# Two attention layers: transposes of a pair's first head ahead of the next pair's scores, softmax weights one block earlier

## The chip, the cores and the metric

The kernel runs on one core of one Trainium2 chip. The metric is the device time of one execution in microseconds (us), median of three runs. The profile is of one more execution on the same core.

## What is computed

A sequence of 16 meta tokens and 256 tokens of width 1024 goes through a first block (feed-forward, an mLSTM mixer, feed-forward) and then through two layers of a second block. The change is in these two layers, which are alike:

```python
for l in range(DEPTH_2):                       # 2 layers
    h = rms_norm(x, pre_norm_g[l]) * (1.0 + scale[:, None, :]) + shift[:, None, :]
    proj = h @ w_in[l]                          # q, k, v, g_att, u, b_gate, c_gate, g_conv
    ...
    att = dilated_attention(q, k, v, rel_bias).astype(h.dtype) * jax.nn.silu(g_att)
    cnv = b_gate * short_conv(c_gate * u, conv_w[l]) * jax.nn.silu(g_conv)
    mix = jnp.concatenate([att, cnv], axis=-1) @ w_out[l]
    x = x + gate[:, None, :] * rms_norm(mix, post_norm_g[l])
```

The dilated attention has 8 heads of 64. Its three windows are folded into one table of biases, so that each head is a softmax over 256 keys: scores, plus bias, exponential, division by the row sum, times v. Everything is float32.

## The kernel before, in words

Activations lie transposed, features on partitions and tokens along the free axis. Each large product is done in three TensorE passes on float32 operands that were split into a high part (`u1`, `w1`) and a low part (`u2`, `w2`). The weights stream from HBM in chunks of 128x1024 (512 KB): SP issues the load into one of five `raw` buffers, ScalarE casts the high part into `w1`, VectorE subtracts it to get the low part `w2`. `advance`, which runs inside `block`, issues cast and subtraction for the chunk that is used four blocks later; there are five buffers of each.

A `block` is one chunk times the normalised activations: 24 matmuls of 128x128 by 128x256 that sum in one of four PSUM banks taken in turn. After q, k and v, the loop that the change touches runs 21 steps, `at_` from 0 to 20; each of steps 0 to 19 has one block: the four gates of the attention first, then for each of four conv groups the blocks u, c_gate, b_gate and g_conv. ScalarE and VectorE empty each block's bank (`sg`, `cu`, `cw`).

Between the blocks stands the attention, by pairs of heads. `k = at_ // 4` counts the pairs and `part = at_ % 4` the step in a pair's four:

- `scores(k)`: TensorE multiplies q and k of both heads into PSUM banks 4 and 7. VectorE adds the bias (`Sb<-ps,Bt`) and takes the row maximum (`st<-Sb`). ScalarE takes four exponentials, and reads four row sums (`Sb,st<-Sb,st` and the accumulator reads).
- `weights2(k)`: VectorE takes the reciprocals of the sums (`st<-st`), GpSimd multiplies them in, two operations for each head (`Sb<-Sb,st`).
- `transposes(h)`: TensorE transposes one head's weights into PSUM bank 5 (`ps<-cs,Sb`), and ScalarE copies them to `PT`. It waits for the weights of the head and for bank 5, which the copy of the head before it frees.
- `values(k)`: TensorE multiplies the transposed weights of both heads by v, and VectorE applies the gate (`at`). `split_mix` then makes high and low parts of it (`m`), the high one on ScalarE, the low one on GpSimd.

In the four steps of pair k (from pair 1 on) TensorE therefore gets: scores of pair k, transposes of the first head of pair k-1, a block; transposes of its second head, a block; a block; `values(k-1)`, a block. Pair 4 has no scores, only the rest of pair 3.

No scheduler moves anything. Every call appends to one list for each engine, and each engine works its list in that order; a wait in a list holds all that stands behind it. A wait whose mark was already waited for is left out. All operations are issued from the lines in `replay`: L112 is an operation that no one waits for, L114 one that raises its engine's semaphore. So rows are told apart by the tiles that they name, not by lines.

Of the kernel before, what the change touches and what calls it, by code (L numbers as in the profile page):

```python
# [116 lines left out]
def build(nc, xT, wst, wada, vec, cst, tab, rb, outT):  # L117
    ctx = ExitStack()
    with ctx:
        def sb(name, shape, dt=F32, c=ctx):  # L120
            return c.enter_context(nc.sbuf_tensor(name, shape, dt))
# [27 lines left out]
        part = sb("part", [P, 96])  # L149
# [117 lines left out]
        def block(x1, x2, n, mid=None, marks=None, ahead=True):  # L267

            if ready:
                return ready.pop(0)  # L270
            b = take()
            c = chunk(ahead)
            pe.wait(free[b])
            for kt in range(KT):
                if marks:
                    pe.wait(marks[kt])
                if mid and kt == KT - 2:
                    mid()
                m = tile_products(ps[:, b, 0:n], c, kt, x1[:, kt, :], x2[:, kt, :], kt == 0, kt == KT - 1,
                                  kt == KT - 1)  # L280
            done_chunk(c, m)
            return b, m
# [822 lines left out]
        def layer(l, ygm, hm):  # L1105
# [51 lines left out]
            def silu2(dst, b, m, w, wr=None):  # L1157

                a = act(partial(nc.scalar.activation, w, ps[:, b, 0:S], ACT.Tanh, scale=0.5), m, wr)
                q = free[b] = dve(partial(nc.vector.scalar_tensor_tensor, dst, w, 1.0, ps[:, b, 0:S], ALU.add,  # L1160
                                                                         ALU.mult), a)
                return q

            def scores(k):


                pe.wait(free[4], free[7], qm[k], qm[4 + k])
                for t in range(2):
                    for e in range(2):
                        hp, b = 64 * e, 4 + 3 * e  # L1170
                        ms = pe(partial(nc.tensor.matmul, ps[:, b, S * t:S * t + S],
                                        qk[hp:hp + 64, k, 128 * t:128 * t + 128], qk[hp:hp + 64, 4 + k, :],
                                        start=True, stop=True))
                dve.wait(ms, br_m["w"])
                for e in range(2):
                    h, i, b = 2 * k + e, (2 * k + e) % 4, 4 + 3 * e
                    dve(partial(nc.vector.scalar_tensor_tensor, Sb[:, i, 0, :], ps[:, b, 0:S], 0.125,
                                Bt[:, h, 0:256], ALU.mult, ALU.add), sbr[i])
                    m = free[b] = dve(partial(nc.vector.scalar_tensor_tensor, Sb[:, i, 1, :], ps[:, b, S:2 * S],
                                              0.125, Bt[:, h, 128:384], ALU.mult, ALU.add))  # L1180
                    m = dve(partial(nc.vector.tensor_reduce, st_[:, i, 0:2], Sb[:, i, :, :], AX_X, ALU.max,
                                    negate=True), m)
                    for t in range(2):
                        x = act(partial(nc.scalar.activation, Sb[:, i, t, :], Sb[:, i, t, :], ACT.Exp,
                                        bias=st_[:, i, t:t + 1], accum_out=st_[:, i, 2 + t:3 + t]), m)
                    ex[h] = x

            def weights2(k):
                for h in (2 * k, 2 * k + 1):
                    i = h % 4  # L1190
                    r_ = dve(partial(nc.vector.reciprocal, st_[:, i, 4:6], st_[:, i, 2:4]), ex[h])
                    for t in range(2):
                        nrm[h] = pool(partial(nc.gpsimd.tensor_scalar, Sb[:, i, t, :], Sb[:, i, t, :],
                                              st_[:, i, 4 + t:5 + t], None, ALU.mult), r_)

            def transposes(h):
                i = h % 4
                pe.wait(free[5], nrm[h])
                for j in range(2):
                    for t in range(2):  # L1200
                        mt = pe(partial(nc.tensor.transpose, 
                            ps[:, 5, S * j + 128 * t:S * j + 128 * t + 128], Sb[:, i, t, 128 * j:128 * j + 128],
                            ident))
                sbr[i] = mt
                ptm[h] = free[5] = act(partial(nc.scalar.copy, PT[:, h % 2, :, :],
                                                          ps[:, 5, :].rearrange("p (j q) -> p j q", q=S)),
                                   mt, ptr[h % 2])

            def values(k):


                pe.wait(ptm[2 * k], ptm[2 * k + 1], mV, free[6])
                for j in range(2):
                    for e in range(2):
                        h, hp = 2 * k + e, 64 * e
                        mo = pe(partial(nc.tensor.matmul, ps[hp:hp + 64, 6, 0:S], Vt[:, j, 64 * h:64 * h + 64],
                                        PT[:, e, j, :], start=j == 0, stop=j == 1, skip_group_check=True))
                ptr[0] = ptr[1] = mo
                dve.wait(mx.get(k - 2))
                m = free[6] = dve(partial(nc.vector.scalar_tensor_tensor,   # L1220
                    at[:, k % 2, :], sg[:, k, :], 0.5, ps[:, 6, S - 1::-1], ALU.mult, ALU.mult), mo, sgm[k])
                todo.append(partial(split_mix, k, at[:, k % 2, :], m))
# [16 lines left out]
            wr = None  # L1239
            for at_ in range(21):  # L1240
                k, part = at_ // 4, at_ % 4
                if part == 0 and k < 4:
                    scores(k)
                if part == 2 and k < 4:
                    weights2(k)
                if part in (0, 1) and 0 < k < 5:
                    transposes(2 * k - 2 + part)
                if part == 3 and 0 < k:
                    values(k - 1)
                while todo:  # L1250
                    todo.pop(0)()
                if at_ == 20:
                    while todo:
                        todo.pop(0)()
                    break
                b, m = block(x1, x2, S)
                if at_ < 4:
                    sgm[at_] = wr = silu2(sg[:, at_, :], b, m, cw_[:, 4, :], wr)
                    continue
                j, part = (at_ - 4) // 4, (at_ - 4) % 4  # L1260
                cwt = lambda tap: vc[:, V_CW2 + 12 * l + 4 * tap + j:V_CW2 + 12 * l + 4 * tap + j + 1]
                if part == 0:
                    cm["u"] = free[b] = act(partial(nc.scalar.copy, cw_[:, 0, :], ps[:, b, 0:S]), m, cm.get("cu"))
                elif part == 1:
                    cm["cu"] = free[b] = dve(partial(nc.vector.tensor_tensor, cu[:, 1:S + 1], cw_[:, 0, :],
                                                     ps[:, b, 0:S], ALU.mult), m, cm["u"], cm.get("t"))
                    m = dve(partial(nc.vector.tensor_scalar, cw_[:, 1, :], cu[:, 0:S], cwt(0), None, ALU.mult),
                            cm["cu"])
                    m = dve(partial(nc.vector.scalar_tensor_tensor, cw_[:, 1, :], cu[:, 1:S + 1], cwt(1),
                                    cw_[:, 1, :], ALU.mult, ALU.add), m)  # L1270
                    cm["t"] = dve(partial(nc.vector.scalar_tensor_tensor, cw_[:, 1, :], cu[:, 2:S + 2], cwt(2),
                                          cw_[:, 1, :], ALU.mult, ALU.add), m)
                elif part == 2:
                    cm["b"] = free[b] = dve(partial(nc.vector.scalar_tensor_tensor, cw_[:, 2, :], cw_[:, 1, :], 0.5,
                                                    ps[:, b, 0:S], ALU.mult, ALU.mult), m, cm["t"], cm.get("x"))
                else:
                    dve.wait(cm.get("p"))
                    wr = silu2(cw_[:, 3, :], b, m, cw_[:, 4, :], wr)
                    m = cm["p"] = pool(partial(nc.gpsimd.tensor_tensor, cw_[:, 2, :], cw_[:, 2, :], cw_[:, 3, :],
                                               ALU.mult), wr, cm["b"])  # L1280
                    cm["x"] = None
                    todo.append(partial(split_conv, j, m))
# [102 lines left out]
```

How the kernel before makes its waits and increments, by code:

```python
    def replay(self, eng):  # L107
        for fn, m in self.ops:
            if fn is None:
                eng.wait_ge(m[0], m[1])
            elif m is None:
                fn()
            else:
                fn().then_inc(m[0], m[1])
```

## Time and profile before

| what | value |
|---|---|
| median of 3 runs | 833.57 us (833.28 to 833.63) |
| profiled execution | 833.62 us, of which the span from first to last instruction is 831.7 us |
| TensorE busy | 803.1 us, 97% of the span |
| VectorE busy | 584.6 us, 70% |
| ScalarE busy | 418.5 us, 50% |
| GpSimd busy | 128.0 us, 15% |
| DMA, all 16 engines | 56.7% of the span for the weights' queue |

Busy times are those of the profile; TensorE's matmuls overlap at their ends, so that the start-to-start distance of two rows says more than the duration of one. A number in square brackets at the end of a row is the time that the engine stood idle ahead of it, and behind the arrow stands what ended that time.

### The profile page before, as it was taken

The page shows a single profiled execution, that of the slowest core. Times are in us where ns is not written, and L with a number is a line of the kernel's source. Part 1 is how long each engine was busy: PE and PEld are TensorE (multiplying, and loading weights), DVE is VectorE, ACT ScalarE, POOL GpSimd, SP SyncE. Part 2 cuts the span into 40 slices and gives each one's busy share as a digit, 9 for nine tenths or more (in the row PEclk, how much of TensorE's full clock was granted, in tenths as well). Part 3 has the DMA queues.
Part 4 walks back from the last instruction along what each step waited for, and adds up shares of the span by engine and source line. Part 5 has one row for each costly group of instructions (what it writes and reads, how often), then busy time and mean ns, then how long its engine had stood idle before and what let it go on. Part 6 is the DMA issues. An engine that isn't in the chain of part 4 may idle for free.

```text
span 831.7 us, 15721 instructions
## 1 busy us (share of the span) xinstructions
PE 803.1 (97%) x6436; PEld 777.6 (93%) x6436; DVE 584.6 (70%) x946; ACT 418.5 (50%) x716; POOL 128.0 (15%) x138
## 2 busy tenths in 40 slices
PE   7999999999999999999999999999999999999996
PEld 7999999999899899999999999989888999898895
DVE  6777776798687875788777768775666468566543
ACT  7544444445257665555444454445654365464541
POOL 3000000032210000010000012220235202025413
PEclk9999999999999999999999999999999999999998
DMA  9876676776245632459888775517444451734421
GB/s 326 295 254 221 226 249 242 226 274 201 88 143 185 196 112 93 152 186 340 291 287 270 275 238 185 184 51 256 150 124 150 154 173 55 259 130 147 131 76 51
DMA packets 45751, 158.96 MB, mean 191 GB/s; under 512 B 5064, under 2 KB 7624, under 8 KB 45680
## 3 DMA queue, kind: packets, MB, share of 16 engines
q1 hardware_dynamic: 45680, 157.96, 56.7%
q8 instruction: 51, 0.84, 0.4%
q14 instruction: 20, 0.16, 0.1%
HBM read 156.88 MB, written 1.06 MB: 190 GB/s over the span
## 4 chain that ended last, share of the span: by engine, by line
PE 76%; DVE 14%; ACT 6%; issue 2%; DMA 1%; POOL 1%; SPq 0%; DVEq 0%; ACTq 0%; POOLq 0%
PE ps L112 69%; PE ps L114 7%; DVE w L114 3%; ACT w L114 2%; DVE u L114 2%; DVE tmp L114 2%; DVE yg L114 1%; DVE Sb L114 1%; DVE st L114 1%; DVE cv L114 1%; ACT SW L114 1%; ACT Sb L114 1%; ACT L114 1%; DMA raw<-wst 1%; POOL rst L114 1%
## 5 line engine op out<-in xcount | busy, mean ns | idle before, releaser
L112 PE MATMUL ps<-u,w 128*128 128x256 f32 (+1 forms) x3887 | 499.9, 285 | 3.1 <-DVE w L114 1.6
L112 PEld LDWEIGHTS ps<-u,w 128*128 128x128 f32 x3887 | 481.9, 188 | 11.3 <-DVE w L114 4.0
L114 DVE TENSOR_TENSOR w<-raw,w 128x1024 fp32r<-128x1024 f32 x245 | 297.4, 1225 | 168.0 <-ACT w L114 161.6
L114 ACT CAST w<-raw 128x1024 fp32r<-128x1024 f32 x245 | 254.8, 1050 | 135.5 <-PE ps L114 124.8
L112 PE MATMUL ps<-h,w 128*128 128x272 f32 (+1 forms) x1000 | 130.4, 285 | 0.0
L112 PEld LDWEIGHTS ps<-h,w 128*128 128x128 f32 x1000 | 126.1, 188 | 0.1
L114 POOL TENSOR_TENSOR sqa<-sqa,sq 128x256 f32<-128x256 f32 (+1 forms) x22 | 23.1, 1050 | 358.3 <-ACT sq L114 357.8
L114 POOL TENSOR_SCALAR Sb<-Sb,st 128x256 f32<-128x256 f32 x32 | 42.9, 1355 | 111.1 <-DVE st L114 111.1
L114 DVE SCALAR_TENSOR_TENSOR acc<-adr,cact,acc 128x1024 f32<-128x1024 f32 x42 | 56.4, 1353 | 0.3 <-DMA adr<-wada 0.3
L114 PE MATMUL ps<-u,w 128*128 128x256 f32 (+1 forms) x169 | 48.1, 284 | 0.0
L112 PE MATMUL ps<-m,w 128*128 128x256 f32 x368 | 46.7, 281 | 0.0
L112 PEld LDWEIGHTS ps<-m,w 128*128 128x128 f32 x368 | 44.8, 188 | 0.0
L114 ACT ACTIVATE sq<-ps 128x256 f32<-128x256 f32 (+1 forms) x37 | 14.4, 390 | 40.4 <-PE ps L114 40.4
L114 PEld LDWEIGHTS ps<-u,w 128*128 128x128 f32 x169 | 32.1, 190 | 0.0
L114 POOL TENSOR_TENSOR rst<-sst,eps 128x2 f32<-128x2 f32 (+2 forms) x7 | 5.6, 802 | 164.3 <-DVE sums L114 155.7
L114 DVE TENSOR_TENSOR hf<-si,ps 128x272 f32<-128x272 f32 (+1 forms) x44 | 18.9, 428 | 15.9 <-ACT si L114 11.4
L114 ACT ACTIVATE si<-tmp 128x272 f32<-128x272 f32 x22 | 9.5, 431 | 38.4 <-DVE tmp L114 38.4
L112 PE MATMUL ps<-y,w 128*128 128x256 f32 x184 | 24.6, 285 | 1.5 <-ACT ytm L114 1.5
L114 ACT ACTIVATE Sb<-Sb,st 128x256 f32<-128x256 f32 x32 | 16.0, 502 | 17.6 <-DVE st L114 17.6
L112 PEld LDWEIGHTS ps<-y,w 128*128 128x128 f32 x184 | 22.8, 188 | 1.7 <-ACT ytm L114 1.7
L114 POOL TENSOR_TENSOR hT<-hT,yg 128x256 f32<-128x256 f32 (+1 forms) x27 | 20.4, 756 | 22.3 <-DVE yg L114 22.3
L114 ACT ACTIVATE si<-ps 128x256 f32<-128x256 f32 x22 | 8.3, 383 | 30.6 <-PE ps L114 29.5
(175 smaller groups left out, 692.2 us busy)
## 6 DMA issues: line engine op xcount, KB each, us to landing
raw<-wst SPq DMA_DIRECT2D x245, 512.0 KB, 4.6
adr<-wada SPq DMA_DIRECT2D x48, 512.0 KB, 4.0
Bt<-bias_rows SPq DMA_DIRECT2D x8, 192.0 KB
hT<-xT SPq DMA_DIRECT2D x4, 272.0 KB, 4.9
outT<-hT SPq DMA_DIRECT2D x2, 384.0 KB, 2.6
outT<-hT SPq DMA_DIRECT2D x1, 256.0 KB, 2.6
cs<-cst SPq DMA_DIRECT2D x1, 140.0 KB, 6.3
cs<-cst SPq DMA_DIRECT2D x1, 128.0 KB, 7.2
```

The source lines that it names most:

```text
L112: fn()
L114: fn().then_inc(m[0], m[1])
```

## The change

It moves two calls in the loop. `transposes` for parts 0 and 1 now stands ahead of `scores`, and `weights2(k)` is called at part 1 rather than part 2, behind the transposes and ahead of the block of that step.

```diff
             for at_ in range(21):
                 k, part = at_ // 4, at_ % 4
+                if part in (0, 1) and 0 < k < 5:
+                    transposes(2 * k - 2 + part)
                 if part == 0 and k < 4:
                     scores(k)
-                if part == 2 and k < 4:
+                if part == 1 and k < 4:
                     weights2(k)
-                if part in (0, 1) and 0 < k < 5:
-                    transposes(2 * k - 2 + part)
                 if part == 3 and 0 < k:
                     values(k - 1)
```

No operation is added or taken away. On TensorE, at the first step of pairs 1, 2 and 3 in each layer, the order of the transposes (`ps<-cs,Sb`) and the scores (`ps<-qk`) is turned; the other rows are blocks:

```order
 L112 MATMUL ps<-u,w 128x256 x23
 L114 MATMUL ps<-u,w 128x256
+L114 MATMUL ps<-cs,Sb 128x128 x4
 L114 MATMUL ps<-qk 128x256 x4
-L114 MATMUL ps<-cs,Sb 128x128 x4
 L112 MATMUL ps<-u,w 128x256 x23
 L114 MATMUL ps<-u,w 128x256
```

The four transposes went from behind the four score products to ahead of them.

On ScalarE, at pair 2 of the first of the two layers, before: the four exponentials (`Sb,st`), the copy of the first head's transposed weights (`PT`), then the cast of a conv result, the cast of a weight chunk, and the second head's copy.

```order
L114 ACTIVATE cw<-ps 128x256
L114 ACTIVATE Sb,st<-Sb,st 128x256 x4
L114 COPY PT<-ps 128x512
L114 CAST m<-cw 128x256
L114 CAST w<-raw 128x1024
```

And the same place in the changed kernel:

```order
L114 ACTIVATE cw<-ps 128x256
L114 COPY PT<-ps 128x512
L114 ACTIVATE Sb,st<-Sb,st 128x256 x4
L114 CAST m<-cw 128x256
L114 CAST w<-raw 128x1024
```

The first head's copy went from behind the exponentials to ahead of them.

On VectorE, between the row maxima of a pair and the conv of that pair's second step, the two reciprocals moved:

```order
 L114 SCALAR_TENSOR_TENSOR Sb0<-ps,Bt 128x256 x2
 L114 TENSOR_REDUCE st0<-Sb0 128x2
-L114 TENSOR_TENSOR w2<-raw,w1 128x1024 x2
+L114 TENSOR_TENSOR w2<-raw,w1 128x1024
+L114 RECIPROCAL st0<-st0 128x2 x2
+L114 TENSOR_TENSOR w2<-raw,w1 128x1024
 L114 TENSOR_TENSOR cu0<-cw0,ps 128x256
 L114 TENSOR_SCALAR cw0<-cu0,vc 128x256
 L114 SCALAR_TENSOR_TENSOR cw0<-cu0,vc,cw0 128x256 x2
-L114 RECIPROCAL st0<-st0 128x2 x2
 L114 TENSOR_TENSOR w2<-raw,w1 128x1024
```

They went from behind the conv of the pair's second step to the place between the weight subtractions of its first and second step. GpSimd's and SP's lists keep their order.

## Rows read from the trace of the kernel before

**Rows 1.** The page: TensorE's busy time, and shares of the chain that ended last.

```profile
PE 803.1 (97%) x6436; PEld 777.6 (93%) x6436; DVE 584.6 (70%) x946; ACT 418.5 (50%) x716; POOL 128.0 (15%) x138
...
PE 76%; DVE 14%; ACT 6%; issue 2%; DMA 1%; POOL 1%; SPq 0%; DVEq 0%; ACTq 0%; POOLq 0%
```

**Rows 2.** TensorE's waits over the whole span: us in total, times, longest.

```profile
PE ps L114 <- ACT PT L114: 6.9, 6, 1.2
PE ps L112 <- DVE dz L114: 5.5, 1, 5.5
```

**Rows 3.** TensorE in order of time, first two steps of pair 2: start, duration, operation.

```profile
612.56 0.28 PE L114 MATMUL ps<-u,w 128*128 128x256 f32 x1
612.77 1.13 PE L114 MATMUL ps<-qk 64*128 64x256 f32 x8
613.83 0.66 PE L114 MATMUL ps<-cs,Sb 128*128 128x128 f32 x4
614.24 2.97 PE L112 MATMUL ps<-u,w 128*128 128x256 f32 x23
617.05 0.28 PE L114 MATMUL ps<-u,w 128*128 128x256 f32 x1
618.48 0.66 PE L114 MATMUL ps<-cs,Sb 128*128 128x128 f32 x4 [1.15 <-ACT PT L114]
618.89 0.84 PE L112 MATMUL ps<-u,w 128*128 128x256 f32 x5
```

**Rows 4.** TensorE in order of time, pair 4, which has transposes but no scores.

```profile
644.58 0.28 PE L114 MATMUL ps<-u,w 128*128 128x256 f32 x1
644.70 0.60 PE L114 MATMUL ps<-cs,Sb 128*128 128x128 f32 x4
645.06 2.97 PE L112 MATMUL ps<-u,w 128*128 128x256 f32 x23
...
648.34 1.90 PE L112 MATMUL ps<-u,w 128*128 128x256 f32 x14
```

**Rows 5.** ScalarE in order of time, pair 2.

```profile
612.87 0.38 ACT L114 ACTIVATE cw<-ps 128x256 f32<-128x256 f32 x1 [1.17 <-PE ps L114]
615.48 0.51 ACT L114 ACTIVATE Sb<-Sb,st 128x256 f32<-128x256 f32 x1 [2.23 <-DVE st L114]
...
617.87 0.56 ACT L114 COPY PT<-ps 128x512 f32<-128x512 f32 x1
618.33 0.40 ACT L114 CAST m<-cw 128x256 fp32r<-128x256 f32 x1
```

**Rows 6.** VectorE in order of time, from the end of pair 1 through pair 2.

```profile
608.14 1.20 DVE L114 TENSOR_TENSOR w<-raw,w 128x1024 fp32r<-128x1024 f32 x1
...
611.74 1.22 DVE L114 TENSOR_TENSOR w<-raw,w 128x1024 fp32r<-128x1024 f32 x1 [1.42 <-ACT w L114]
613.29 0.42 DVE L114 SCALAR_TENSOR_TENSOR cw<-cw,ps 128x256 f32<-128x256 f32 x1 [0.33 <-ACT cw L114]
613.97 0.75 DVE L114 SCALAR_TENSOR_TENSOR Sb<-ps,Bt 128x256 f32<-128x256 f32 x2 [0.26 <-PE ps L114]
...
619.72 1.23 DVE L114 TENSOR_TENSOR w<-raw,w 128x1024 fp32r<-128x1024 f32 x1 [2.89 <-ACT w L114]
...
624.32 0.22 DVE L114 RECIPROCAL st<-st 128x2 f32<-128x2 f32 x2
...
627.75 1.23 DVE L114 TENSOR_TENSOR w<-raw,w 128x1024 fp32r<-128x1024 f32 x1 [1.42 <-ACT w L114]
```

**Rows 7.** GpSimd in order of time, merged: the four multiplications of pair 1.

```profile
608.25 5.50 POOL L114 TENSOR_SCALAR Sb<-Sb,st 128x256 f32<-128x256 f32 x4 [9.06 <-DVE st L114]
```

**Rows 8.** The second of these four, and all 32 of both layers (duration ns min/median/max).

```profile
610.12 0.92 POOL L114 TENSOR_SCALAR Sb<-Sb,st 128x256 f32<-128x256 f32 x1
...
L114 POOL TENSOR_SCALAR Sb<-Sb,st x32: 920/1224/1974, 593.6 to 784.6; 128x256 f32<-128x256 f32 x32
```

**Rows 9.** Busy time by stretch: the four steps of pair 2 (columns PE, PEld, DVE, ACT, POOL, PEclk, DMA share, GB/s).

```profile
612.68:628.69 16.01, 14.86 (x122) 13.49 (x120) 10.46 (x20) 8.41 (x18) 7.32 (x8) 1.00 0.40 130
```

## The prediction

> **What bounds the kernel now.** I read the page first: TensorE is busy for 97% of the span and carries 76% of the chain that ended last [rows 1]. So a change is worth what it does to TensorE's list, and the first question is where TensorE still waits. The table of its waits answers that: the largest entry is one of 6.9 us in six equal pieces of at most 1.2 us, always for ScalarE's copy to `PT`; the next, 5.5 us, is one single wait for another tile [rows 2]. Six is three pairs times two layers.
>
> The list of TensorE in order of time shows one of the six. In pair 2 the scores start at 612.77, the first head's transposes at 613.83, a block at 614.24; the second head's transposes then wait, TensorE idle for 1.15 us, and start at 618.48 [rows 3]. ScalarE's list tells why: the copy that frees bank 5 starts only at 617.87, behind four exponentials that begin at 615.48 and wait for VectorE's row maxima [rows 5]. The transposes that it copies had ended at 613.83 + 0.66 = 614.49 [rows 3]. So the copy lay ready for 3.4 us behind work that has nothing to do with it. Pair 4 has no scores, hence no exponentials, and there the same two groups of transposes run without a wait [rows 4]. The granted clock in this stretch is 1.00, the higher level (2.4 GHz) [rows 9]; TensorE had been busy ahead of it, and with less idle time I see no reason for it to fall.
>
> **The wait that goes.** I cost it by start-to-start distances, since durations overlap. From the block of the first step to that of the second it is 618.89 - 614.24 = 4.65 us [rows 3]; the same step in pair 4, with the same transposes and block, takes 648.34 - 645.06 = 3.28 us [rows 4]. The difference, 1.37 us, is more than the 1.15 us that the wait's own row gives, because that row counts from the modelled end of the last matmul. Six times 1.37 is 8.2 us; six times 1.15 is 6.9 us. I take 8.2, as it compares like with like, and keep 6.9 as the bound.
>
> Does it go whole? In the changed order the transposes start at 612.56 + 0.12 (the distance from 644.58 to 644.70 [rows 4]) = 612.68 and end 0.60 later, at 613.28. ScalarE finishes the activation of the block before at 613.25 [rows 5], so the copy runs from about 613.3 to 613.9. The second head's transposes are due behind the next block, at 617.05 + 0.12 = 617.17 [rows 3]. That is 3.3 us to spare.
>
> **The turned order on TensorE.** Before, from the last matmul of a block to the first of the next one it is 614.24 - 612.56 = 1.68 us: 0.21 to the scores, 1.06 to the transposes, 0.41 to the block [rows 3]. In pair 4 the transposes follow at 0.12 and take 0.36 [rows 4]. So going into the scores costs 0.21 - 0.12 = 0.09 more than going into other work, and coming out of them 0.41 - 0.36 = 0.05. Turned: 0.12 + 0.36 + 0.09 + 1.06 + 0.05 = 1.68. I cost it at nothing. No row shows scores right behind transposes. At worst the transposes run out before the scores begin: 0.66 long at a distance of 0.41 [rows 3], 0.25 each, 1.5 us for six. At best both small prices vanish: 0.14 each, 0.8 us.
>
> **The copy and the scores on ScalarE and VectorE.** The scores come 612.68 + 0.36 + 0.09 - 612.77 = 0.36 us later, and so do bias, maxima and exponentials. In return the copy, 618.33 - 617.87 = 0.46 us, no longer stands behind them [rows 5]. The cast that follows moves from 618.33 to about 618.2; the rest of the pair on both engines keeps its times to 0.1 us. But TensorE arrives 1.37 us earlier at the next pair. VectorE's last weight subtraction of the pair ends at 627.75 + 1.23 = 628.98 [rows 6], and the emptying of a block's bank, 0.42 us as at 613.29, stands between it and the bias of the scores. The next scores end at about 629.0: those before ended by 613.97, plus 0.36 for the turned order, plus a pair of 16.01 - 1.37 [rows 6, 9]. So VectorE starts on them some 0.3 us late, at most 1 us over three pairs. What this lateness could reach is the weights: the subtraction at 619.72 to 620.95 [rows 6] serves the first block of the next pair, at 614.24 + 16.01 = 630.25 [rows 3, 9]. It is 9.3 us early, and 7.9 after the change. It hides the lateness easily. The pair 4 steps, without score work, let both engines catch up before the loop ends.
>
> **The weights a block sooner.** VectorE's two reciprocals move from 624.32 to about 621.0, behind the subtraction that ends at 620.95 [rows 6]. They need the row sums; ScalarE takes these ahead of the very cast which that subtraction waits for, so VectorE cannot be held there. If it were, the pair's second subtraction and the conv behind it would wait, and TensorE for them, but with a lead of about 8 us between. GpSimd starts 3.3 us earlier. Its list is unchanged. Even unmoved, the first head's two operations end at 610.12 + 0.92 = 611.04 [rows 8], ahead of the 612.68 at which the transposes will now want them; moved, with all operations as long as the longest (1.97 us [rows 8]), they would end at 621.1 + 3.9 = 625.0, and the transposes are due at 612.68 + 16.01 - 1.37 = 627.32. So this edit buys nothing by itself; it widens a margin. No DMA is moved, and SP's list stays. The loads follow TensorE's pace; the DMA share in the stretch is 0.40 [rows 9].
>
> In the new place GpSimd works beside other VectorE operations. A multiplication that started at 608.25, 0.11 us behind a weight subtraction, took 610.12 - 608.25 = 1.87 us, where the next took 0.92 [rows 6 to 8]. The subtraction at 611.74 began while GpSimd's four were running (608.25 to 613.75) and took 1.22 us, as the one at 619.72 did ahead of the next four [rows 6, 7]. So GpSimd gives way and VectorE does not.
> The Trainium skill, page "SBUF — State Buffer", section "Who interferes with whom", says that a VectorE instruction with two SBUF inputs and a GpSimd instruction that reads SBUF share a read interface, and that whichever issues first holds it for its whole length while the other blocks fully. The first of my two observations agrees with it, the second does not. By the rule VectorE too would be held, up to four times a pair; that is the last rival below.
>
> **Sum.** 833.62 (the profiled execution; the median, 833.57, is 0.05 lower) - 8.2 + 0 = 825.4 us.
>
> **Rivals.**
> - *The smaller gain.* The wait is worth only 6.9 us, giving 826.7, or transposes also run out before scores, 1.5 us more: 828.2. For it: no row shows that order. Against: pair 4's distances.
> - *The change doesn't do what it says.* The second head's transposes still wait, because ScalarE comes late to the copy. It would have to be 3.3 us late for any wait and 4.7 us late for all of the old one. Ahead of the activation at 612.87 it idles for 1.17 us [rows 5], so it is early now. The time would be 829.5 with half of the wait left, 833.6 with all.
> - *Slower: VectorE is held by GpSimd.* If each of GpSimd's four multiplications held a VectorE operation for its own median length of 1.22 us [rows 8], VectorE would fall back 4.9 us a pair, 14.6 over three; the weights' lead of 7.9 takes up the first part, and 6.7 us a layer would reach TensorE: 825.4 + 13.4 = 838.8. It decides from a hold of (7.9 + 4.1) / 12 = 1.0 us each, where the loss equals the gain. Against it: the 1.22 us subtraction beside a busy GpSimd.
>
> **Chances.** Forecast 0.73, smaller gain 0.16, wait stays 0.07, slower 0.04. The range goes from 833.62 - 8.2 - 0.8 = 824.6 to the end of the smaller gain, 828.2; it leaves out the last two. About 0.2% (1.7 us) is what a measurement of this kernel can tell from no change. Faster takes the first two cases and over half of the third: 0.93; the rest of that, 0.03, is no change; slower 0.04.
>
> **What would show it.** Right: TensorE's table of waits loses the 6.9 us entry; the second step of pairs 1 to 3 takes 3.28 us, the first keeps 1.68 between blocks; a pair takes 14.6 us where it took 16.01; ScalarE's copy stands ahead of the exponentials and ends about 1.2 us behind the block; GpSimd's four start about 3.3 us earlier in their pair; VectorE's subtractions stay at 1.23 us. Wrong: waits of TensorE for `w`, `Sb` or `PT` in these steps, scores starting more than 0.1 us behind the transposes' 0.36, or subtractions of 2 us.

## The result, and the profile after

The changed kernel takes 825.34 us (median of five runs, 825.07 to 825.68), the kernel before beside it 833.36 us (832.94 to 833.63). That is 8.02 us less, a ratio of 0.9903 (95% interval 0.9892 to 0.9915). The profiled execution went from 833.62 to 825.59 us, its span from 831.7 to 823.7.

TensorE's table of waits begins after the change with the entry that stood second before [rows 2]; the 6.9 us for `PT` are gone from it, and nothing for `Sb` or `w` has grown in its place (the entry for `rst` was 2.4 us in four waits before; its new wait lies between the two layers, outside these steps):

```profile
PE ps L112 <- DVE dz L114: 5.7, 1, 5.7
PE ps L114 <- POOL rst L114: 3.1, 5, 0.7
PE ps L112 <- ACT ytm L114: 1.5, 1, 1.5
PE ps L112 <- DVE w L114: 1.3, 4, 0.4
```

TensorE in order of time after the change, the first two steps of pair 3 (start, duration, operation), which answers to [rows 3]:

```profile
626.07 0.28 PE L114 MATMUL ps<-u,w 128*128 128x256 f32 x1
626.20 0.60 PE L114 MATMUL ps<-cs,Sb 128*128 128x128 f32 x4
626.73 1.13 PE L114 MATMUL ps<-qk 64*128 64x256 f32 x8
627.79 2.99 PE L112 MATMUL ps<-u,w 128*128 128x256 f32 x23
630.61 0.28 PE L114 MATMUL ps<-u,w 128*128 128x256 f32 x1
630.74 0.60 PE L114 MATMUL ps<-cs,Sb 128*128 128x128 f32 x4
631.09 2.95 PE L112 MATMUL ps<-u,w 128*128 128x256 f32 x23
```

The second head's transposes start 0.13 us behind the block's last matmul started, with no wait. The step between the two blocks takes 631.09 - 627.79 = 3.30 us where it took 4.65. Between the blocks of the first step lie 627.79 - 626.07 = 1.72 us, where it was 1.68.

ScalarE in pair 2 after the change, which answers to [rows 5]:

```profile
611.70 0.38 ACT L114 ACTIVATE cw<-ps 128x256 f32<-128x256 f32 x1
612.14 0.59 ACT L114 COPY PT<-ps 128x512 f32<-128x512 f32 x1
614.75 0.51 ACT L114 ACTIVATE Sb<-Sb,st 128x256 f32<-128x256 f32 x1 [2.02 <-DVE st L114]
...
617.13 0.39 ACT L114 CAST m<-cw 128x256 fp32r<-128x256 f32 x1
```

The copy now starts as soon as its transposes are done, fills idle time ahead of the exponentials, and ends at 612.73. The second head's transposes come at 616.04, 3.3 us later.

Busy time by stretch, the four steps of pair 2 after the change, for [rows 9]:

```profile
611.50:626.20 14.70, 14.70 (x123) 13.49 (x122) 10.66 (x19) 8.10 (x19) 7.38 (x8) 1.00 0.48 142
```

A pair takes 14.70 us where it took 16.01, and TensorE is busy through all of it. That is 1.31 us a pair, 7.9 for six, against 8.0 in the span: nearly the whole difference lies here.

### The profile page after: what moved, and what is told of

Same layout as the page of the kernel before. It is cut to its first block, busy times and chain, and to the rows that moved or that the text cites. A ratio compares the mean times of both kernels' runs of the same rounds, so it can differ in the third digit from the quotient of the medians.

```text
span 823.7 us, 15721 instructions
## 1 busy us (share of the span) xinstructions
PE 801.0 (97%) x6436; PEld 776.4 (94%) x6436; DVE 586.2 (71%) x946; ACT 417.6 (51%) x716; POOL 130.2 (16%) x138
## 3 DMA queue, kind: packets, MB, share of 16 engines
HBM read 156.88 MB, written 1.06 MB: 192 GB/s over the span
## 4 chain that ended last, share of the span: by engine, by line
PE 78%; DVE 12%; ACT 6%; issue 2%; POOL 1%; DMA 0%; SPq 0%; DVEq 0%; ACTq 0%; POOLq 0%
PE ps L112 71%; PE ps L114 7%; DVE w L114 3%; DVE u L114 2%; ACT w L114 2%; DVE tmp L114 2%; DVE yg L114 1%; DVE cv L114 1%; ACT SW L114 1%; POOL rst L114 1%; ACT L114 1%; ACT ytm L114 1%; DMA hT<-xT 0%; DVE Vs L114 0%; ACT u L114 0%
## 5 line engine op out<-in xcount | busy, mean ns | idle before, releaser
L114 POOL TENSOR_SCALAR Sb<-Sb,st 128x256 f32<-128x256 f32 x32 | 45.0, 1423 | 89.1 <-DVE st L114 89.1
```

Of the source, the lines that this page charges most:

```text
L114: fn().then_inc(m[0], m[1])
```

## The experiments

| run | median us | ratio to before | 95% interval |
|---|---|---|---|
| the change | 825.34 | 0.9903 | 0.9892 to 0.9915 |
| transposes ahead, weights not sooner | 827.49 | 0.9932 | 0.9919 to 0.9944 |
| weights sooner, transposes not ahead | 833.12 | 0.9999 | 0.9990 to 1.0008 |
| copy first on ScalarE only | 824.83 | 0.9902 | 0.9888 to 0.9915 |
| copy between the heads' exponentials | 825.47 | 0.9906 | 0.9891 to 0.9921 |
| second head in a bank of its own | 827.00 | 0.9928 | 0.9915 to 0.9940 |
| weights two blocks later than the change | 830.54 | 0.9964 | 0.9952 to 0.9977 |
| copy first, and weights sooner | 825.27 | 0.9902 | 0.9889 to 0.9916 |
| copy behind the weight cast | 842.63 | 1.0110 | 1.0091 to 1.0130 |
| weights sooner for pair 0 alone | 825.74 | 0.9907 | 0.9894 to 0.9920 |

The kernel before had medians of 833.08 to 833.52 us beside these runs. Theory T is that of the prediction: the copy to `PT`, held behind exponentials on ScalarE, kept bank 5 from the second head's transposes. Its rivals are that the sooner weights bring the gain (R1), that the turned order on TensorE does (R2), and that the second head's transposes would have waited for something else anyway (R3).

**The two halves of the change apart.** First the transposes alone, the changed kernel with:

```diff
-                if part == 1 and k < 4:
+                if part == 2 and k < 4:
                     weights2(k)
```

> Transposes ahead of the scores as in the change, the weights left at the pair's third step as before. Theory T (the whole gain is the copy to PT that no longer stands behind the exponentials): TensorE loses its 6.9 us of waits for PT, as in the changed kernel. The prediction said that the sooner weights buy nothing, so about 825.3. Against that, from the trace after: GpSimd's four of pair 2 start at 619.91 there; behind the conv they would start near 623.6 and the first head would be ready 2.8 us later, at 626.4, where its transposes are due at 626.20. So a wait of TensorE for Sb of 0.2 to 0.6 us a pair may appear, 826 to 828 in all. Rival R1 (the gain comes from the sooner weights): 833.4, as before.

It took 827.49 us, 5.6 us less than the kernel before beside it. So R1 is out as the source of the whole gain. But 2.2 us of the change's 8.0 are missing. GpSimd's first two multiplications of pair 0, then TensorE in order of time at pair 1, in this run:

```profile
593.68 1.81 POOL L114 TENSOR_SCALAR Sb<-Sb,st 128x256 f32<-128x256 f32 x1 [36.52 <-DVE st L114]
595.48 1.97 POOL L114 TENSOR_SCALAR Sb<-Sb,st 128x256 f32<-128x256 f32 x1
```

```profile
596.60 0.28 PE L114 MATMUL ps<-u,w 128*128 128x256 f32 x1
597.59 0.63 PE L114 MATMUL ps<-cs,Sb 128*128 128x128 f32 x4 [0.72 <-POOL Sb L114]
```

The first head of pair 0 is ready at 597.45, its transposes could have started at 596.72. They wait 0.87 us by start distances, in each of the two layers, and now the scores wait behind them: 1.7 of the 2.2 us. I had expected a wait in every pair; at the later pairs none is listed.

Then the weights alone, the kernel before with:

```diff
-                if part == 2 and k < 4:
+                if part == 1 and k < 4:
                     weights2(k)
```

> Weights a block sooner as in the change, scores ahead of the transposes as before. T: the copy still waits behind the exponentials, six waits of 1.15 us stay, 833.4 within 0.3. R1: about 825.3.

833.12 us, with the same entry in TensorE's table of waits as before:

```profile
PE ps L114 <- ACT PT L114: 6.9, 6, 1.2
```

So the sooner weights alone are worth nothing.

**Only ScalarE's order.** TensorE keeps scores ahead of transposes; `mid` puts the first head's transposes into the lists behind the score products, so that ScalarE gets the copy ahead of the exponentials. The kernel before with:

```diff
-            def scores(k):
+            def scores(k, mid=None):
...
+                if mid:
+                    mid()
                 dve.wait(ms, br_m["w"])
...
-                    scores(k)
+                    scores(k, partial(transposes, 2 * k - 2) if k else None)
...
-                if part in (0, 1) and 0 < k < 5:
+                if part in (0, 1) and 0 < k < 5 and (part or k == 4):
                     transposes(2 * k - 2 + part)
```

> The kernel before with one move, on ScalarE alone: the copy of the first head's transposed weights goes ahead of the four exponentials. TensorE's list (scores, then transposes) and the weights stay as before. T: the wait goes as in the changed kernel, 8.0 us, and the 0.04 us a pair that the turned order cost on TensorE are not paid: 825.0 to 825.4. Rival R2 (the gain needs the turned order on TensorE): 833.4.

824.83 us, 0.2 below the expected range: one moved copy gives the whole gain, without the turned order and without the sooner weights. R2 is out. With the weights a block sooner on top of it:

```diff
-                if part == 2 and k < 4:
+                if part == 1 and k < 4:
                     weights2(k)
```

> The copy first on ScalarE with TensorE's old order (scores, then transposes), and the weights at the second step as in the change. T: as the changed kernel or up to 0.5 us below it, 824.9 to 825.4, since the scores come 0.4 us sooner and the two changes of shape on TensorE cost as before. If the turned order is worth something of its own, it is above 825.4.

825.27 us. The three versions, the change and these two, lie within each other's intervals; none is shown to be better than the change.

**More and less of the delay.** The copy between the two heads' exponentials (the same `mid`, called in the loop behind the first head's):

```diff
                     ex[h] = x
+                    if mid and e == 0:
+                        mid()
```

> The kernel before, with the copy to PT between the two heads' exponentials on ScalarE: half of the old delay. T: in the times of before the first head's exponentials and reads end at 616.6, the copy at about 617.2; the second head's transposes are due at 617.17. So the wait nearly goes, 0 to 0.2 us a pair: 825.2 to 826.5. A gain in proportion to the exponentials passed would give half of it, 829.4.

825.47 us, the whole gain again and no wait for `PT` in the table. Half of the delay costs nothing: in pair 2 of this run the copy ends at 615.32, and the second head's transposes start at 615.44, when they are due. And more delay, the copy kept back until the block's weight cast is issued (`copy` is the copy to `PT`, in `transposes`; the lower part stands in the loop):

```diff
+                if h % 2 == 0 and h < 6:
+                    copies.append(copy)
+                else:
+                    copy()
...
                 b, m = block(x1, x2, S)
+                while copies:
+                    copies.pop(0)()
```

> The kernel before, with the first head's copy to PT put still further back on ScalarE: behind the cast of the block's weight chunk (and, in pairs 2 and 3, of a conv result) too. T: the copy comes 0.95 us later in pair 1 and 1.3 us later in pairs 2 and 3 (the starts of these casts in the trace of before), so TensorE's waits for PT grow from 6.9 to about 14 us and the time from 833.4 to 840 to 841. If the wait were bounded by something else than the copy, the time would stay near 833.4.

842.63 us, of runs from 840.12 to 846.32: more than the expected 840 to 841. The waits are as expected, 13.8 us in six:

```profile
PE ps L114 <- ACT PT L114: 13.8, 6, 2.4
```

The rest is TensorE's clock. Its list at pair 2 in this run, and the busy time of the stretch from 621.0 to 626.2 and of a part of it (columns as in [rows 9]):

```profile
618.40 0.28 PE L114 MATMUL ps<-u,w 128*128 128x256 f32 x1
621.08 0.66 PE L114 MATMUL ps<-cs,Sb 128*128 128x128 f32 x4 [2.40 <-ACT PT L114]
621.49 4.48 PE L112 MATMUL ps<-u,w 128*128 128x256 f32 x23
```

```profile
621.00:626.20 5.20, 5.12 (x31) 5.12 (x32) 2.10 (x3) 1.84 (x5) 0.00 (x0) 0.67 0.48 128
622.50:625.50 3.00, 3.00 (x16) 3.00 (x15) 1.22 (x1) 0.80 (x1) 0.00 (x0) 0.50 0.57 175
```

Behind the wait of 2.40 us the block's 23 matmuls take 4.48 us instead of 2.97, at a mean granted clock of 0.67 of full speed: from 622.5 to 625.5 it was 0.50, the lower level (1.2 GHz), and the rest of the stretch is mostly at the higher one (2.4 GHz). In the profiled execution this happened behind three of the six waits, with blocks of 4.48, 4.00 and 4.42 us: 12.90 - 3 x 2.97 = 4.0 us. With 13.8 - 6.9 = 6.9 us more of waits that is 10.9 of the 11.5 us by which its span of 843.2 exceeds 831.7.

**What the transposes waited for.** Every order as before, but the second head's transposes write one of the four rotating banks, in `transposes`:

```diff
-                pe.wait(free[5], nrm[h])
+                b = take() if h % 2 else 5
+                pe.wait(free[b], nrm[h])
...
-                ptm[h] = free[5] = act(partial(nc.scalar.copy, PT[:, h % 2, :, :],
+                ptm[h] = free[b] = act(partial(nc.scalar.copy, PT[:, h % 2, :, :],
```

> The kernel before, with every order as it was, but the second head's transposes write one of the four rotating banks and not bank 5. The copy to PT still ends as late as before. T: what the transposes waited for was bank 5 alone, so the wait goes: 825 to 826. Rival R3 (the second head's transposes would wait for its weights or for another thing anyway): 833.4, or a part of it.

827.00 us, above the expected 825 to 826. The wait for `PT` is gone although the copy comes as late as ever. In pair 2 of this run the second head's transposes start before the first head's copy does:

```profile
615.54 0.60 PE L114 MATMUL ps<-cs,Sb 128*128 128x128 f32 x4
616.55 0.56 ACT L114 COPY PT<-ps 128x512 f32<-128x512 f32 x1
```

So the wait was for the bank; R3 is out for these steps. What is missing is a new wait at pair 4, once a layer. GpSimd and TensorE in this run:

```profile
638.52 3.67 POOL L114 TENSOR_SCALAR Sb<-Sb,st 128x256 f32<-128x256 f32 x3 [5.02 <-DVE st L114]
```

```profile
640.20 0.28 PE L114 MATMUL ps<-u,w 128*128 128x256 f32 x1
641.34 0.66 PE L114 MATMUL ps<-cs,Sb 128*128 128x128 f32 x4 [0.86 <-POOL Sb L114]
```

Pair 4 has no scores ahead of its transposes, and TensorE, no longer held in the pairs before, comes to them before GpSimd is done with the first head. In this run the weights stand at the third step, as before the change. With the copy first they stood there too, and no wait for `Sb` came. The copy's place makes the difference as far as the rows show it: VectorE waits 2.89 us for the weight cast behind the late copy in pair 2 (until 618.40) and 2.41 us with the copy first, and GpSimd's last two groups of multiplications in the first layer start 15.25 us apart here (623.27 and 638.52), 14.75 there. So the late copy holds more than the bank.

**The margin of the weights.** The weights later than in the change, at part 3:

```diff
-                if part == 1 and k < 4:
+                if part == 3 and k < 4:
                     weights2(k)
```

> The changed kernel with the weights two blocks later than in it, at the pair's fourth step. It measures the margin which the sooner weights give. From the trace after: reciprocals near 624.9 in pair 2, GpSimd from 625.1, the first head ready at 627.0 to 627.9, transposes due at 626.20, so TensorE waits 0.8 to 1.7 us six times for Sb: 830 to 835.5. If the margin of 2.3 us that the prediction worked out for slow multiplications held here too: 825.3.

830.54 us, at the lower end of the expected range. TensorE's table of waits of this run has six waits, but shorter ones than the 0.8 to 1.7 us that I expected:

```profile
PE ps L114 <- POOL Sb L114: 3.2, 6, 0.9
```

They stand at pairs 1, 3 and 4 of each layer. By start distances the first head's transposes come 1.0 us late at pair 1, 0.2 at pair 2 and 0.5 at pairs 3 and 4: 4.6 us in both layers, of the 5.2 us that this run is slower than the change.

And which weights have to be sooner, the changed kernel with:

```diff
-                if part == 1 and k < 4:
+                if part == (1 if k == 0 else 2) and k < 4:
                     weights2(k)
```

> The changed kernel, with the weights of pair 0 alone a block sooner and those of pairs 1 to 3 at the third step as before. In the run with all weights late TensorE waited for Sb once a layer, 0.72 us at pair 1, for the weights of pair 0. If that is where the sooner weights pay, the table of waits shows none for Sb and most of the 2 us come back: 825.4 to 826.3. If the three later pairs pay for it as well: 827 or more.

825.74 us, within the interval of the change and with no wait for `Sb` in the table. What the transposes alone had lost was pair 0's; pairs 1 to 3 don't need the sooner weights.

## Why the prediction was right, step by step

- **The wait.** Sized by start distances at 1.37 us a pair; it measured 4.65 - 3.30 = 1.35. The wait's own row, 1.15 us, would have given 826.7, outside the five runs. Runs with only the copy moved, with half the delay, with twice the wait and with another bank all agree on the cause.
- **The turned order.** Costed at nothing, it cost 1.72 - 1.68 = 0.04 us a pair. The scores start 0.53 us behind the transposes, where I had worked out 0.45; the transposes don't run out before them, which would have been 0.25 more. One of my signs of being wrong did come up here: the scores start 0.17 us behind the transposes' 0.36, and I had named 0.1. It costs little because the way out of the scores into the block, 627.79 - 626.73 = 1.06 us, lacks the 0.05 that I had added. That the two nearly cancel was luck.
- **ScalarE's and VectorE's lateness.** In pair 2 VectorE begins on the scores' bias 1.74 us behind the start of the transposes, in pair 3 2.02 us, now without idle time ahead of it: 0.28 later, as worked out. VectorE in order of time after the change, at the bias of pair 2 and the first subtraction behind it:

```profile
613.24 0.75 DVE L114 SCALAR_TENSOR_TENSOR Sb<-ps,Bt 128x256 f32<-128x256 f32 x2
...
618.51 1.23 DVE L114 TENSOR_TENSOR w<-raw,w 128x1024 fp32r<-128x1024 f32 x1 [2.42 <-ACT w L114]
```

  That subtraction ends at 619.74 and serves the block at 627.79, 8.05 us ahead, for an expected 7.9.
- **The weights: this step failed, though the time does not show it.** I wrote that the edit buys nothing by itself and that even unmoved the first head's multiplications end early enough. The first half holds: alone it moved nothing. The second was read from pair 1 [rows 7, 8] and taken for all pairs. In pair 0 the first two multiplications are slow ones, 1.81 and 1.97 us instead of 1.87 and 0.92, and end 0.7 us too late for the turned order. The trace of before had the row:

```profile
595.42 1.97 POOL L114 TENSOR_SCALAR Sb<-Sb,st 128x256 f32<-128x256 f32 x1
```

  It ends at 597.39, and the transposes of pair 1, ahead of the scores, would there have been due 0.12 us behind the block's last matmul at 596.54. Each of the two began 0.05 to 0.2 us behind a weight subtraction of VectorE (593.43 and 595.37 in that trace). Since the change has both edits, the sum came out right; of its 8 us, 2.2 hang on the sooner weights, those of pair 0 as far as the runs can tell (825.74 us with these alone sooner).
- **GpSimd and VectorE: this reading was too simple.** I read that GpSimd gives way and VectorE does not, from a subtraction at 611.74 that kept its 1.22 us. GpSimd's multiplication beside it (611.02, 0.92 us long) then had only 0.20 us left, so that row could hardly show it. After the change there are better ones. VectorE in pair 2, then GpSimd's first two multiplications there (their spans are rough):

```profile
620.20 1.26 DVE L114 TENSOR_TENSOR w<-raw,w 128x1024 fp32r<-128x1024 f32 x1 [0.33 <-ACT w L114]
621.83 0.57 DVE L114 TENSOR_SCALAR cw<-cu,vc 128x256 f32<-128x256 f32 x1
```

```profile
619.91 0.93 POOL L114 TENSOR_SCALAR Sb<-Sb,st 128x256 f32<-128x256 f32 x1 [1.56 <-DVE st L114]
620.81 1.44 POOL L114 TENSOR_SCALAR Sb<-Sb,st 128x256 f32<-128x256 f32 x1
```

  The subtraction begins with 0.64 us of the first multiplication to go and takes 1.26 us, 0.03 more than the 1.23 of before: there the reading held. It did not hold for the conv's multiplication by its first tap, which begins with 0.42 us of the second one to go. VectorE's rows for it before and after, and GpSimd's multiplications after (duration ns min/median/max):

```profile
L114 DVE TENSOR_SCALAR cw<-cu,vc x8: 352/353/355, 606.7 to 792.3; 128x256 f32<-128x256 f32 x8
```

```profile
L114 DVE TENSOR_SCALAR cw<-cu,vc x8: 354/570/574, 606.8 to 785.0; 128x256 f32<-128x256 f32 x8
L114 POOL TENSOR_SCALAR Sb<-Sb,st x32: 922/1441/2212, 592.3 to 774.3; 128x256 f32<-128x256 f32 x32
```

  VectorE loses 0.22 us there and 0.1 in the two conv operations behind it, GpSimd 0.22 in its median and 0.24 in its longest. All are far from the 1.0 us a multiplication from which the slower rival would have decided, and all are hidden. The rule of the Trainium skill ("SBUF — State Buffer", "Who interferes with whom") that the two can hold each other, in either direction, agrees with this. That the one that comes second blocks until the other ends does not show for the subtraction, which lost 0.03 us with 0.64 to go.

## What to carry to other kernels

When an engine that works in order serves two purposes, look for the short operation that frees a buffer and stands behind long ones that wait for something else; moving it forward costs nothing where the engine idles anyway. Size such a wait by comparing start-to-start distances with a place where the same work runs freely, not by the idle time of its row. And when a step is pulled ahead of another, read the margin of its own inputs in each repetition, the first and the last above all.

## What had not been expected of the hardware

TensorE's granted clock stayed at 1.00 with single waits of 1.15 us in a pair of 16 us, and fell in the run with the copy behind the weight cast: behind three of its four waits of 2.4 us and neither of its two of 2.1 us. TensorE had been busy for some 15 us ahead of the first wait of 2.4 us, and just as long ahead of the one that no fall followed. Two of the stretches behind a fall had a mean of 0.67 and 0.70 of full speed (621.0 to 626.2 and 639.8 to 645.0). That run's times spread over 6.2 us, those of the other experiments over 0.6 to 1.1. Why the clock fell behind three of the four waits and not behind the fourth is open. The Trainium skill ("TensorE: Matmul & The Clock Gate", "What's actually happening") says that the array's clock falls to half when it has been idle. The rows agree in this: 0.50 from 622.5 to 625.5, 1.00 ahead of the wait, and each fall behind idle time.
